# Two transformer blocks on one core: the 31-tap convolution as 64 four-tap matrices from memory, and the query block moved to the end of the input stage

## The chip, the cores and the metric

The kernel runs on one core of one Trainium2 chip. The metric is device time in microseconds (us) of one execution. The engines are named as in the profile: PE (TensorE), DVE (VectorE), ACT (ScalarE), POOL (GpSimd) and SP (SyncE, which here issues all DMAs). PEld is PE's weight load.

## The reference, cut to what matters

The kernel computes a first block of two layers and a second, different block of two layers, on 256 tokens of width 1024. The change is in the first block alone, between its input projection and its output projection:

```python
a = rmsnorm(h, norm_mix_pre[i])
u = einsum('bsd,de->bse', a, w_in[i])
q, k, v, qi, ki, wi, u_conv, u_pool = split(u)     # 512,128,128,1024,64,16,512,256
q, k, qi, ki = partial_rope(...)                   # first 16 of each 64 features
# index scores: relu(qi . ki) weighted by wi, summed over 16 heads; top 64 keys of each token
# attention of 8 heads over the selected keys
a_, g = split(u_conv)                              # 256 and 256
y = a_ * sigmoid(g)
y = depthwise causal convolution of y with 31 taps, 256 channels; + conv_b
y_conv = silu(layernorm(y)) @ conv_pw              # 256 x 256
# y_pool: window means over 2, 4, 8, 16 tokens less the input, then four 64 x 64 matrices
mix = concat([y_attn, y_conv, y_pool]) @ w_out
```

## The kernel before, in words

**Weights.** All weights stream through one queue of chunks of 128 x 2048 numbers, in the order in which they are used. SP loads each chunk in two halves of 512 KB into `raw` (two slots); ACT copies a half to `whi` in the reduced format fp32r (`prep`, line 490), DVE subtracts to get the rest `wlo` (`lo`, line 946); both have four slots. SP's load of chunk s waits for `lo` of chunk s-2, and `prep` of chunk s waits until PE is done with chunk s-4. A product of full precision is then three matmuls: high by high, high by low, low by high. `wide_block` does this with 512 columns of weights moving and 128 tokens as the stationary operand; `tile` does it with the weights stationary and 256 tokens moving. Products that don't involve streamed weights are plain fp32 matmuls, which the trace shows as two instructions each.

**Order.** Each engine has one program, written out by hand, and runs it in order; semaphores join them. Banks of PSUM (`acc` 0 to 3, `ub` 0 to 3) are handed on by `fill(bank, event)`: the next user of a bank waits for the event that the last use was given. In layer L of the first block the chunks are, counted from s0: 0 and 1 index key, key, value and the index weights; 2 to 5 the index queries; 6 and 7 the queries (`block_in(3, ...)`, by token halves into banks acc 2 and 3); 8 and 9 the convolution's input, 10 the pooling's (`pair_in`); then 11 to 14 the output projection ("out 0" to "out 3") and 15 on the feed-forward ("ffn 0" on).

**The stage of the change.** PE interleaves chunks 6 to 8 with the dots of the 16 index heads. ACT takes each head's relu, DVE adds it to the index sum (`index_sums`, line 1084). DVE rotates the queries (`rope(3)`, line 1073 on) in the middle of the index sums, and gates the convolution's input by ACT's sigmoid (`gated`) after the last index sum and in the search. The search for the 64 largest is eight rounds of MAX8 and MATCH_REPLACE8 (lines 1130, 1133). PE meanwhile runs chunk 9, turns the queries (`turn_in(3)`), runs chunk 10, the scores of heads 0 and 1, and 14 taps. Then comes a loop over eight heads: turn the probabilities (line 1891), scores of head hh+2 (lines 1818, 1819), values of head hh-1 (lines 1903 to 1907), and some taps. DVE masks the scores and takes the row maximum (lines 1152, 1156), ACT the exponent (line 637) and the copy of the turned probabilities (line 645).

**The convolution.** Channels lie on partitions, tokens along the row (`YC`, two units of 128 channels). A tap is a matmul of a diagonal 128 x 128 matrix with 256 shifted tokens (line 1929). POOL makes the diagonals, 46 a layer, in a ring of 16 (line 415), after the index dots, because they lie where the index queries lay; between the first 30 and the last 16 it does the pooling's window sums (lines 427 to 441). DVE does the other 16 taps itself (lines 1184, 1186), and a matmul by the identity adds them (line 1947). Mean, variance, spread of the reciprocal deviation and the pointwise convolution (lines 1953, 1968, 1977, 1987) follow on PE late in the loop and in the output projection.

## Time and profile before

| | |
|---|---|
| median of 3 runs | 2365.07 us (2364.63 to 2365.8) |
| the profiled execution: its time, its span | 2364.69 us, 2362.9 us |
| PE busy, PEld busy | 2336.6 us (99%), 1981.5 us (84%) |
| DVE, ACT, POOL busy | 1550.3 (66%), 1194.3 (51%), 118.8 (5%) us |
| granted TensorE clock | 9 (90% or more) in all 40 slices |
| HBM read | 424.05 MB, 180 GB/s over the span |
| chain that ended last | PE 88%, DVE 6%, POOL 2%, DMA 1%, ACT 1% |

The time of an execution is that of the whole program; the span runs from the first to the last instruction that the profile records. A matmul's record is longer than its slot, since matmuls are pipelined: what it costs in a row of them is the distance of the starts. A row with "x28" stands for 28 instructions in a row, its length reaches from the first's start to the last's modelled end. "[0.92 <-POOL ...]" is idle time before the row and what ended it.

### The profile page before, as it was taken

How to read it: one execution, taken by the hardware profiler on the slowest of the kernel's cores; microseconds unless marked ns; L12 is line 12 of the kernel's file. 1: busy time of each engine (PE TensorE's matmuls, PEld its weight loads, DVE VectorE, ACT ScalarE, POOL GpSimd, SP SyncE). 2: the span in 40 equal slices, each digit the busy share in tenths (PEclk: the TensorE clock that was granted, in tenths of full speed). 3: DMA queues.
4: the chain of work that ended last, by engine and by line, in shares of the span. 5: the costliest groups of instructions: out<-in, count | busy, mean ns of one | idle time of the engine just before them, and what ended most of it. 6: DMA issues, size and time to landing. Idle time of an engine off the chain costs nothing.

```text
span 2362.9 us, 30405 instructions
## 1 busy us (share of the span) xinstructions
PE 2336.6 (99%) x12096; PEld 1981.5 (84%) x12096; DVE 1550.3 (66%) x2041; ACT 1194.3 (51%) x1734; POOL 118.8 (5%) x223
## 2 busy tenths in 40 slices
PE   7999999999999999999999999999999999999998
PEld 6888888888888888988888888888889888888887
DVE  6866567866656656776485666665567765856664
ACT  6445446445445546545344455554565454444553
POOL 0500000500000000000000000000000000000000
PEclk9999999999999999999999999999999999999999
DMA  7236656236556665554656465565565445564563
GB/s 273 81 104 205 208 187 213 73 108 214 185 175 227 198 196 179 195 167 159 199 178 202 160 213 180 179 229 195 182 196 193 160 165 191 182 207 162 190 194 126
DMA packets 117501, 427.11 MB, mean 181 GB/s; under 512 B 13296, under 2 KB 13552, under 8 KB 117104
## 3 DMA queue, kind: packets, MB, share of 16 engines
q1 hardware_dynamic: 117360, 425.16, 54.7%
q8 instruction: 97, 1.59, 0.3%
q14 instruction: 44, 0.36, 0.0%
HBM read 424.05 MB, written 1.05 MB: 180 GB/s over the span
## 4 chain that ended last, share of the span: by engine, by line
PE 88%; DVE 6%; POOL 2%; DMA 1%; ACT 1%; issue 1%; SPq 0%; DVEq 0%; POOLq 0%; ACTq 0%
PE ub L1632 21%; PE ub L1636 11%; PE ub L1610 8%; PE ub L1612 8%; PE ub L1611 8%; PE acc L1610 8%; PE acc L1612 8%; PE acc L1611 8%; DVE wlo L946 2%; DMA raw<-in_w 1%; PE acc L1929 1%; POOL tapd L415 1%; DVE XN L987 1%; PE acc L2042 1%; ACT junk L512 1%
## 5 line engine op out<-in xcount | busy, mean ns | idle before, releaser
L946 DVE TENSOR_TENSOR wlo<-raw,whi 128x1024 fp32r<-128x1024 f32 x776 | 916.7, 1222 | 246.1 <-ACT whi L490 244.2
L490 ACT ACTIVATE whi<-raw 128x1024 fp32r<-128x1024 f32 x776 | 782.8, 1053 | 259.4 <-PE ub L1612 148.5
L1632 PE MATMUL ub<-xhl,whi 128*128 128x512 f32 x2176 | 595.2, 395 | 0.0
L1632 PEld LDWEIGHTS ub<-xhl,whi 128*128 128x128 f32 x2176 | 375.5, 189 | 53.5 <-issue 1.0
L1636 PEld LDWEIGHTS ub<-xhl,wlo 128*128 128x128 f32 x2176 | 333.5, 189 | 46.2
L1636 PE MATMUL ub<-xhl,wlo 128*128 128x256 f32 x2176 | 345.8, 281 | 0.0
L1610 PE MATMUL acc<-whi,bhl 128*128 128x512 f32 x736 | 288.6, 392 | 0.0
L1612 PE MATMUL acc<-whi,bhl 128*128 128x512 f32 x736 | 287.5, 391 | 0.0
L1611 PE MATMUL acc<-wlo,bhl 128*128 128x512 f32 x736 | 287.2, 390 | 0.0
L1610 PE MATMUL ub<-whi,xhl 128*128 128x512 f32 (+1 forms) x704 | 275.6, 391 | 7.8 <-DVE wlo L946 4.3
L1611 PE MATMUL ub<-wlo,xhl 128*128 128x512 f32 (+1 forms) x704 | 272.8, 387 | 0.0
L1612 PE MATMUL ub<-whi,xhl 128*128 128x512 f32 (+1 forms) x704 | 272.7, 387 | 0.0
L1610 PEld LDWEIGHTS ub<-whi,xhl 128*128 128x128 f32 x704 | 132.8, 189 | 36.5 <-DVE wlo L946 6.4
L1612 PEld LDWEIGHTS acc<-whi,bhl 128*128 128x128 f32 x736 | 138.1, 188 | 29.3
L1611 PEld LDWEIGHTS acc<-wlo,bhl 128*128 128x128 f32 x736 | 138.2, 188 | 27.4
L1610 PEld LDWEIGHTS acc<-whi,bhl 128*128 128x128 f32 x736 | 138.2, 188 | 27.1
L1612 PEld LDWEIGHTS ub<-whi,xhl 128*128 128x128 f32 x704 | 132.8, 189 | 26.6
L1611 PEld LDWEIGHTS ub<-wlo,xhl 128*128 128x128 f32 x704 | 132.9, 189 | 25.3
L1348 DVE TENSOR_TENSOR tX<-tS,ub 128x512 f32<-128x512 f32 x72 | 49.5, 688 | 137.3 <-ACT tS L773 136.8
L773 ACT ACTIVATE tS<-ub 128x512 f32<-128x512 f32 x72 | 42.9, 596 | 151.3 <-PE ub L1636 151.2
L1610 PE MATMUL ub<-whi,bhl 128*128 128x512 f32 x256 | 99.8, 390 | 0.0
L1612 PE MATMUL ub<-whi,bhl 128*128 128x512 f32 x256 | 99.6, 389 | 0.0
(311 smaller groups left out, 2578.5 us busy)
## 6 DMA issues: line engine op xcount, KB each, us to landing
raw<-in_w SPq DMA_DIRECT2D x776, 512.0 KB, 4.9
gain<-in_gains SPq DMA_DIRECT2D x20, 512.0 KB, 8.2
par<-in_par SPq DMA_DIRECT2D x2, 1068.0 KB, 9.4
DEC<-in_decay SPq DMA_DIRECT2D x2, 768.0 KB, 7.3
H<-in_x SPq DMA_DIRECT2D x2, 512.0 KB, 6.1
out_h<-H SPq DMA_DIRECT2D x4, 256.0 KB, 2.3
par<-in_par SPq DMA_DIRECT2D x2, 419.0 KB, 8.2
PT<-in_p SPq DMA_DIRECT2D x2, 256.0 KB, 8.4
```

The source lines that it names most:

```text
L415: do(pool.tensor_scalar(tapd[:, n % TAP_RING, :], ident, par1[:, P1["dw"] + n:P1["dw"] + n + 1], 1.0, ALU.mult, ALU.mult), taps)
L490: do(act.activation(whi[:, s % RING, c], raw[:, s % RAW, c], ACT.Copy), counts["w_hi"])
L512: do(act.activation(junk[:, :], H[:, t, fcol(fb)], ACT.Square, scale=1.0 / 32, accum_out=ssh[:, t, fb:fb + 1]), counts["ssh"])
L773: do(act.activation(units(tS[:, j % 2, :]), ub[:, 2 * (j % 2):2 * (j % 2) + 2, 0:S], ACT.Copy), counts["a_out"])
L946: do(dve.tensor_tensor(wlo[:, s % RING, c], raw[:, s % RAW, c], whi[:, s % RING, c].bitcast(f32), ALU.subtract), counts["w_lo"])
L987: do(dve.scalar_tensor_tensor(XN[:, fcol(fb)], H[:, t, fcol(fb)], rh[:, t:t + 1], gain[:, 1, fcol(fb)], ALU.mult, ALU.mult), counts["xn_re ...
L1348: do(dve.tensor_tensor(units(tX[:, j % 2, :]), units(tS[:, j % 2, :]), ub[:, 2 * (j % 2):2 * (j % 2) + 2, S:2 * S], ALU.add), counts["us"])
L1610: pe.matmul(o, x_h, w_h, start=first, stop=False, skip_group_check=True)
L1611: pe.matmul(o, x_h, w_l, start=False, stop=False, skip_group_check=True)
L1612: return pe.matmul(o, x_l, w_h, start=False, stop=last, skip_group_check=True)
L1632: pe.matmul(bank, whi[:, s % RING, n:n + P], xhl[:, kt, :, :].rearrange("p a n -> p (a n)"), start=kt == 0, stop=False, skip_group_check=True)
L1636: last = pe.matmul(bank[:, S:], wlo[:, s % RING, n:n + P], xhl[:, kt, 0, :], start=False, stop=kt == KT - 1, skip_group_check=True)
```

## The change

- The depthwise convolution is done for 64 channels at a time. Partitions 0 to 63 hold their even tokens, 64 to 127 their odd ones, each shifted by pairs: `YC` has four groups of 128 pairs. One 128 x 128 matrix, made on the host (`shifts`), holds up to four taps' entries: from even and odd input tokens to even and odd output tokens. Sixteen such matmuls of 128 columns make a group, 64 a layer. POOL's diagonals, DVE's own taps and the matmul that added them are gone.
- The matrices come from memory, in eight pieces of 512 KB a layer, through SP's queue and into a ring of four, two of which lie where the index queries and one where a projected block lay. SP waits, in its order, for those to be free and for earlier pieces to be used.
- The convolution's input is projected by token halves (`conv_in`, wide matmuls) from chunks 6 and 7, the pooling's from chunk 8, and the queries from chunks 9 and 10. The gated result is laid down by tokens (each 64 channels twice), turned by eight transposes (`turn_conv`), and ACT takes even tokens to the lower and odd tokens to the upper partitions (`even_and_odd`).
- DVE gates earlier, hands the pooling's input to POOL before the last three index sums, and rotates the queries after the search.
- PE's order after the dots: `turn_conv`, the query block, 14 taps, `turn_in(3)`, 10 taps, scores of heads 0 and 1, then the loop with 8 taps in each of the first five heads.
- Mean, variance, spread and pointwise convolution go by four groups of 128 columns. The variance comes out with tokens on partitions. The pointwise product uses 64 rows at a time, even tokens into bank ub 0 and odd into ub 1.

```diff
-TAP_RING = 16
+GROUPS = 4
+SHIFTS = 16
+PIECE = 8
+PIECES = GROUPS * SHIFTS // PIECE
+TAP_RING = 4
+PAIRS = S // 2
 RSPAN = 384
-TAPS_DVE = 16
-TAPS_BEFORE, TAPS_AFTER = 14, (7, 7, 6, 6, 6)
+TAPS_BEFORE, TAPS_AFTER = 24, (8, 8, 8, 8, 8)
...
-        tapd = sb("tapd", 0, at=unit(12), shape=[P, TAP_RING, P])
+        tapw = [sb(f"tapw{n}", 0, at=unit(u), shape=[P, PIECE, P]) for n, u in enumerate((32, 4, 12, 16))]
...
+        def load_taps(L, first, end):
+            for n in range(first, end):
+                k = PIECES * L + n
+                if n >= TAP_RING:
+                    sp.wait_ge(sem["tap_used"], k - TAP_RING + 1)
+                sp.dma_start(tapw[n % TAP_RING][:, :, :].rearrange("p a n -> p (a n)"),
+                             a["taps"][k * P:(k + 1) * P, :]).then_inc(sem[f"tap_in{n % TAP_RING}"], 16)
...
+                if s == s1(L, "inp", 10):
+                    if L:
+                        sp.wait_ge(sem["split_free"], s1(L - 1, "ple") + 1)
+                    load_taps(L, 0, 1)
+                if s == s1(L, "out", 2):
+                    sp.wait_ge(sem["ze"], 7 * L + 5)
+                    load_taps(L, 1, 2)
+                    sp.wait_ge(sem["dots_done"], IDX_HEADS * (L + 1))
+                    load_taps(L, 2, 5)
+                if s == s1(L, "out", 3):
+                    load_taps(L, 5, 6)
+                if s == s1(L, "ffn"):
+                    load_taps(L, 6, PIECES)
...
-            def tap_diagonals(start, end):
-                for n in range(start, end):
-                    if n >= TAP_RING:
-                        pool.wait_ge(sem["tap_used"], L * (2 * TAPS - TAPS_DVE) + n - TAP_RING + 1)
-                    do(pool.tensor_scalar(tapd[:, n % TAP_RING, :], ident,
-                                          par1[:, P1["dw"] + n:P1["dw"] + n + 1], 1.0, ALU.mult, ALU.mult), taps)
...
-            def sigmoid(f):
-                used(s0 + 8 + f)
-                do(act.activation(tS[:, f, 0:S], acc[:, f, S:2 * S], ACT.Sigmoid), counts["act_out"])
+            def sigmoid(t):
+                if t:
+                    used(s0 + 7)
+                else:
+                    nxt("cz")
+                do(act.activation(tS[:, t, 0:S], acc[:, 3 * t, S:2 * S], ACT.Sigmoid), counts["act_out"])
+            def even_and_odd(b):
+                nxt("yt_done")
+                for i in range(2):
+                    r = slice(64 * i, 64 * i + 64)
+                    src = acc[r, b, :].rearrange("p (g m i) -> p g m i", g=2, i=2)[:, :, :, i]
+                    do(act.activation(YC[r, 2 * b:2 * b + 2, SHIFTS - 1:], src, ACT.Copy),
+                       counts["yc_ready"] if i else None)
...
-            relus(4, 10)
+            relus(4, 7)
+            sigmoid(0)
+            relus(7, 10)
+            sigmoid(1)
             prep(s0 + 11)
+            relus(10, 16)
+            even_and_odd(0)
+            even_and_odd(1)
+            prep(s0 + 12)
             copy(3, 0)
+            prep(s0 + 13)
             copy(3, 1)
-            relus(10, 13)
-            sigmoid(0)
-            relus(13, 16)
-            prep(s0 + 12)
-            sigmoid(1)
-            prep(s0 + 13)
             turned_in(3)
...
-            def gated(f):
+            def gated(t):
                 nxt("act_out")
                 settle()
-                do(dve.tensor_tensor(YC[:, f, TAPS - 1:], acc[:, f, 0:S], tS[:, f, 0:S], ALU.mult),
-                   counts["in_free"])
+                x, y = (z.rearrange("p (g d) -> p g d", d=64).unsqueeze(2).broadcast_to([P, GROUPS, 2, 64])
+                        for z in (acc[:, 3 * t, 0:S], tS[:, t, 0:S]))
+                do(dve.tensor_tensor(YT[:, t, :, :, :], x, y, ALU.mult), counts["in_free"])
...
-            index_sums(4, 10)
+            index_sums(4, 7)
+            gated(0)
+            index_sums(7, 10)
+            gated(1)
             lo(s0 + 11)
-            rope(3)
-            index_sums(10, 16)
+            index_sums(10, 13)
             dve.wait_ge(sem["pads_ready"], L + 1)
-            gated(0)
+            used(s0 + 8)
+            do(dve.tensor_copy(UP[:, :, 16:], units(acc[:, 2, :])), counts["in_free"])
+            settle()
+            do(dve.memset(small[:, 0, 2:3], 0.0), counts["pool_in"])
+            index_sums(13, 16)
...
-                if r == 3:
-                    gated(1)
-            used(s0 + 10)
-            do(dve.tensor_copy(UP[:, :, 16:], units(acc[:, 2, :])), counts["in_free"])
-            settle()
-            do(dve.memset(small[:, 0, 2:3], 0.0), counts["pool_in"])
+            rope(3)
...
-            def own_taps(first, end):
-                for k in range(first, end):
-                    w = par1[:, P1["dw"] + TAPS + k:P1["dw"] + TAPS + k + 1]
-                    y = YC[:, 1, k:k + S]
-                    settle()
-                    if k == TAPS - TAPS_DVE:
-                        do(dve.tensor_scalar(CD[:, 0, :], y, w, None, ALU.mult))
-                    else:
-                        do(dve.scalar_tensor_tensor(CD[:, 0, :], y, w, CD[:, 0, :], ALU.mult, ALU.add),
-                           counts["cd_ready"] if k == TAPS - 1 else None)
...
+                    do(dve.tensor_scalar(cvar[:, :], acc[:, 3, 0:2], LN_EPS, None, ALU.add), counts["var_ready"])
...
+            do(dve.tensor_copy(spread[:, :, :], crs[:, :].unsqueeze(2).broadcast_to([P, 2, 64])),
+               counts["spread_ready"])
...
+            def conv_in(part, t):
+                s = s0 + 6 + part
+                if part == 0:
+                    fill(A_[3 * t], "in_free")
+                last = wide_block(s, 4 * part, t, acc[:, 3 * t, :], part == 0, part == 1, xhi, xlo)
+                if t:
+                    give(last)
+                elif part:
+                    give(last, "cz")
+            def pool_in(f):
+                arrive(s0 + 8, f)
                 if f == 0:
-                    fill(A_[n], "in_free")
+                    fill(A_[2], "in_free")
                 for kt in range(KT):
-                    last = tile(acc[:, n, f * S:(f + 1) * S], xhl[:, kt, :, :], s, f * KT + kt,
+                    last = tile(acc[:, 2, f * S:(f + 1) * S], xhl[:, kt, :, :], s0 + 8, f * KT + kt,
                                 kt == 0, kt == KT - 1)
                 if f:
                     give(last)
+            def turn_conv():
+                pe.wait_ge(sem["in_free"], 3 * L + 2)
+                for b in range(2):
+                    fill(A_[b], "yc_ready")
+                    for g in (2 * b, 2 * b + 1):
+                        for t in range(2):
+                            c = (g % 2) * S + t * P
+                            last = pe.transpose(acc[:, b, c:c + P],
+                                                YT[:, t, g, :, :].rearrange("p a d -> p (a d)"), ident)
+                    give(last, "yt_done")
...
-            block_in(3, 0, 0)
+            conv_in(0, 0)
             dots(0, 2)
-            give(block_in(3, 0, 1))
+            conv_in(0, 1)
             dots(2, 4)
             turn_in(2)
-            give(block_in(3, 1, 0), "xz")
+            conv_in(1, 0)
             dots(4, 7)
-            give(block_in(3, 1, 1))
+            conv_in(1, 1)
             dots(7, 10)
-            pair_in(s0 + 8, 0, 0)
+            pool_in(0)
             dots(10, 13)
-            pair_in(s0 + 8, 0, 1)
+            pool_in(1)
             dots(13, 16)
-            for f in range(2):
-                pair_in(s0 + 9, 1, f)
-            turn_in(3)
-            for f in range(2):
-                pair_in(s0 + 10, 2, f)
+            turn_conv()
+            both(3, 0)
+            both(3, 1)
...
             def taps(count):
                 for n in range(taken[0], taken[0] + count):
-                    f, k = divmod(n, TAPS)
+                    g, q = divmod(n, SHIFTS)
+                    piece, k = divmod(n, PIECE)
                     if n == 0:
                         fill(A_[3], "c_ready")
+                    if n % (2 * SHIFTS) == 0:
+                        pe.wait_ge(sem["yc_ready"], 2 * L + g // 2 + 1)
                     if k == 0:
-                        pe.wait_ge(sem["in_free"], 3 * L + 1 + f)
-                    pe.wait_ge(sem["tap_ready"], L * (2 * TAPS - TAPS_DVE) + n + 1)
-                    give(pe.matmul(acc[:, 3, f * S:(f + 1) * S], tapd[:, n % TAP_RING, :],
-                                   YC[:, f, k:k + S], start=k == 0, stop=f == 0 and k == TAPS - 1),
-                         "tap_used")
+                        pe.wait_ge(sem[f"tap_in{piece % TAP_RING}"], 16 * (2 * L + piece // TAP_RING + 1))
+                    last = pe.matmul(acc[:, 3, cols(g)], tapw[piece % TAP_RING][:, k, :], YC[:, g, q:q + PAIRS],
+                                     start=q == 0, stop=q == SHIFTS - 1)
+                    if k == PIECE - 1:
+                        give(last, "tap_used")
                 taken[0] += count
+            taps(TAPS_BEFORE - 10)
+            turn_in(3)
+            taps(10)
...
-                if hh == 4:
-                    nxt("cd_ready")
-                    give(pe.matmul(acc[:, 3, S:2 * S], ident, CD[:, 0, :], start=False, stop=True), "conv_done")
...
-                U_[1].take(pe, sem["prod_ready"], 4 * L + 4)
+                for place_ in U_[0:2]:
+                    place_.take(pe, sem["prod_ready"], 4 * L + 4)
                 for f in range(2):
-                    for k in range(2):
-                        c = P1["conv_pw"] + (k * 2 + f) * P
-                        last = pe.matmul(ub[:, 1, f * S:(f + 1) * S], par1[:, c:c + P], cact[:, k, :],
-                                         start=k == 0, stop=k == 1)
+                    for g in range(GROUPS):
+                        for j in range(2):
+                            r = slice(64 * j, 64 * j + 64)
+                            c = P1["conv_pw"] + (g * 2 + f) * P
+                            last = pe.matmul(ub[:, j, f * PAIRS:(f + 1) * PAIRS], par1[r, c:c + P],
+                                             cact[r, g, :], start=g == 0, stop=g == GROUPS - 1)
...
+def shifts(dw):
+    out = np.zeros((GROUPS, SHIFTS, 2, 64, 2, 64), np.float32)
+    c = np.arange(64)
+    for q in range(SHIFTS):
+        for i in range(2):
+            for j in range(2):
+                k = 2 * q + i - j
+                if 0 <= k < TAPS:
+                    out[:, q, i, c, j, c] = dw[k].reshape(GROUPS, 64)
+    out = out.reshape(PIECES, PIECE, P, P).transpose(0, 2, 1, 3)
+    return np.ascontiguousarray(out).reshape(PIECES * P, PIECE * P)
```

## Rows read from the trace of the kernel before

**Rows 1.** The page's busy time and share of the span by engine.
```profile
PE 2336.6 (99%) x12096; PEld 1981.5 (84%) x12096; DVE 1550.3 (66%) x2041; ACT 1194.3 (51%) x1734; POOL 118.8 (5%) x223
```

**Rows 2.** PE's waits, whole span: for whom; us in total, times, longest us.
```profile
PE acc L1929 <- POOL tapd L415: 1.8, 2, 0.9
```

**Rows 3.** PE's timeline, wide matmuls: start us, length us, engine, line, operation, count.
```profile
59.62 0.39 PE L1610 MATMUL acc<-whi,xhl 128*128 128x512 f32 x1
...
60.30 0.39 PE L1610 MATMUL acc<-whi,xhl 128*128 128x512 f32 x1
```

**Rows 4.** Timeline of PE from the index scores to head 5.
```profile
76.63 0.35 PE L1617 MATMUL acc<-xhl,whi 128*128 128x256 f32 x1 [0.40 <-ACT sm L590]
...
82.45 1.03 PE L1813 MATMUL ub<-cst,ZA 128*128 128x128 f32 x8
83.24 0.36 PE L1617 MATMUL acc<-xhl,whi 128*128 128x256 f32 x1
...
89.17 0.50 PE L1818 MATMUL ub<-KK,Q 64*128 64x128 f32 x4
...
90.03 6.31 PE L1929 MATMUL acc<-YC,tapd 128*128 128x256 f32 x28
96.19 0.49 PE L1891 MATMUL ub<-cst,sm 128*128 128x128 f32 x3
...
100.58 0.49 PE L1891 MATMUL ub<-cst,sm 128*128 128x128 f32 x3
...
102.57 3.24 PE L1929 MATMUL acc<-YC,tapd 128*128 128x256 f32 x14
...
121.35 0.49 PE L1891 MATMUL ub<-cst,sm 128*128 128x128 f32 x3
```

**Rows 5.** Timeline of PE in the second block: a head's scores and what follows.
```profile
1049.35 1.47 PE L2053 MATMUL acc<-q,k 128*128 128x256 f32 x8
1050.58 0.48 PE L1610 MATMUL ub<-whi,xhl 128*128 128x512 f32 x1
```

**Rows 6.** Timeline of VectorE: rotation, index sums, search, mask.
```profile
71.83 0.43 DVE L1073 TENSOR_TENSOR tX<-ZA,cc 128x256 f32<-128x256 f32 x1
...
73.22 2.45 DVE L1084 SCALAR_TENSOR_TENSOR iacc<-sm,wi,iacc 128x128 f32<-128x128 f32 x6
76.14 2.60 DVE L1084 SCALAR_TENSOR_TENSOR iacc<-sm,wi,iacc 128x128 f32<-128x128 f32 x6 [0.47 <-ACT sm L590]
...
79.33 0.62 DVE L1130 MAX8 best<-iacc 128x8 f32<-128x128 f32 x2
...
91.26 0.68 DVE L1138 COPY UP<-acc 128x512 f32<-128x512 f32 x1
...
93.15 0.56 DVE L1152 SCALAR_TENSOR_TENSOR sm<-ub,bias 128x384 f32<-128x384 f32 x1
```

**Rows 7.** POOL and VectorE together; third row: a line's ns min/median/max.
```profile
99.92 1.08 POOL L429 TENSOR_TENSOR W<-W 128x538 f32<-128x538 f32 x1
100.03 1.25 DVE L1186 SCALAR_TENSOR_TENSOR CD<-YC,par,CD 128x256 f32<-128x256 f32 x1
L1186 DVE SCALAR_TENSOR_TENSOR CD<-YC,par,CD x30: 483/485/1369, 100.0 to 466.7; 128x256 f32<-128x256 f32 x30
103.58 0.72 POOL L438 TENSOR_TENSOR PO<-W,cst 64x256 f32<-64x256 f32 x1
```

**Rows 8.** Timeline of ScalarE: two copies of a bank, end of head 0's exponent.
```profile
69.50 1.09 ACT L565 ACTIVATE ZA<-acc 128x512 f32<-128x512 f32 x2
...
95.19 0.18 ACT L637 ACTIVATION_READ_ACCUMULATOR sm<-sm,rmax 128x1 f32 x1
```

**Rows 9.** The page's DMA issues: count, KB each, median us to landing.
```profile
raw<-in_w SPq DMA_DIRECT2D x776, 512.0 KB, 4.9
```

**Rows 10.** Timeline of PE near the start: matmuls of 336 columns.
```profile
14.07 0.48 PE L1611 MATMUL ub<-wlo,xhl 128*128 128x336 f32 x1
14.35 0.48 PE L1612 MATMUL ub<-whi,xhl 128*128 128x336 f32 x1
```

More of the change, by code:

```diff
@@ L1951, in _ @@
                             fill(A_[3], "ha_ready")
-                            for k in range(2):
-                                last = pe.matmul(acc[:, 3, 0:S], means[:, :], cacc[:, k, :], start=k == 0, stop=k == 1)
+                            for g in range(GROUPS):
+                                last = pe.matmul(acc[:, 3, 0:PAIRS], means[:, :], cacc[:, g, :],
+                                                 start=g == 0, stop=g == GROUPS - 1)
                             give(last, "mean_done")
@@ L1966, in _ @@
                             fill(A_[3], "var_ready")
-                            for k in range(2):
-                                last = pe.matmul(acc[:, 3, 0:S], means[:, :], tS[:, 0, k * S:(k + 1) * S], start=k == 0, stop=k == 1)
+                            for g in range(GROUPS):
+                                last = pe.matmul(acc[:, 3, 0:2], tS[:, 0, cols(g)], means[:, 0:P:64],
+                                                 start=g == 0, stop=g == GROUPS - 1)
                             give(last, "stat_done")
@@ L1974, in last_values @@
                         turn_values(1)
-                        nxt("diag_ready")
+                        nxt("spread_ready")
                         fill(A_[3], "ha_ready")
-                        give(pe.matmul(rb, means[:, :], diag[:, :, :].rearrange("p a b -> p (a b)"), start=True, stop=True),
+                        give(pe.matmul(rb, spread[:, :, :].rearrange("p a b -> p (a b)"), ident, start=True, stop=True),
                              "rb_ready")
@@ L2250, in lay_out @@
         w_out = w_out.reshape(KT, P, D)[list(OUT_ORDER)].reshape(D, D)
-        w += [block_chunks(m) for m in (first, qi[:, 0:512], qi[:, 512:], q)]
-        w += [chunks(tiles(np.concatenate(last, axis=1))), column_chunks(w_out)]
+        w += [block_chunks(m) for m in (first, qi[:, 0:512], qi[:, 512:], conv)]
+        w += [chunks(tiles(pool)), block_chunks(q), column_chunks(w_out)]
         w += in_order({"first": block_chunks(v["w_up"][l][:, 0:1024]), "up": chunks(tiles(v["w_up"][l])),
@@ L2298, in lay_out @@
         "p": np.concatenate(ps, axis=0),
+        "taps": np.concatenate(taps, axis=0),
         "w": np.ascontiguousarray(np.concatenate(w, axis=0).reshape(-1, CHUNK)),
```

105 lines of the change are left out of this document (44 added, 61 removed).

## Prediction

> **What bounds the kernel now.** I read the page first: PE is busy for 99% of the span [rows 1]. A busy PE need not be a full one, so next came PE's waits. In the stretch that the change touches there are two a layer: 0.92 us for a diagonal that POOL makes [rows 2] and 0.40 us for an index relu [rows 4]. So PE's order of work is the clock of this kernel. A microsecond of PE work saved between the index scores and the out projection is a microsecond of the whole, as long as no other engine's result is late for PE. Last I read the timeline of each engine from 56 to 132 us, where the first layer does all this. The second layer repeats it with the same spacings (the wait on POOL has the same length in both [rows 2]), so I work out one layer and double it.
>
> **Prices.** A 512-column matmul of split numbers starts every 0.227 us (three in 0.68) [rows 3]; a 256-column one costs 0.123 (48 from 83.24 to 89.17, refill included) [rows 4]. A full-precision matmul is two instructions; with 256 columns each takes 0.22 (28 in 6.16 us) [rows 4]. With 128 columns: eight instructions of the second block's scores, four of 256 and four of 128 columns, take 1.23 us until the next matmul starts [rows 5]; less 4 x 0.22 that leaves 0.09 each. The weights must be loaded for each, and 0.12 is what a 256-column split matmul, as long in columns streamed, needs with its load. Ends 0.09 and 0.12; I take 0.108. A transpose costs 0.10 (eight in 0.79) [rows 4].
>
> **Up to the first softmax turn.** Before, PE is done with the index scores at 76.23 (76.63 less the wait) and begins turning head 0's probabilities at 96.19, a span of 19.96 us [rows 4]. What precedes 76.23 is the same work in other banks (four wide quarter blocks, one chunk of narrow tiles, 16 heads of dots), and I cost it at nothing. After it, one layer does this:
> - eight transposes of the gated convolution, 0.8, plus 0.1 for the switch: 77.15. The 0.40 us wait on the relu is covered by the first four.
> - 48 wide matmuls of the query block in place of two chunks of 48 narrow ones: 10.9 + 0.1, to 88.15 (the narrow ones took 11.9).
> - The taps write bank 3, which the second token half of the query block has just filled. They wait for ScalarE to copy it out: 0.28 until the last matmul lands beyond its slot, 0.55 for the copy (two in 1.09) [rows 8], and the semaphore. 0.9, a new wait: 89.05.
> - 14 taps, 28 x 0.108 = 3.0: 92.05.
> - Then the query block must be turned, and for that VectorE must have rotated it, which the change puts behind the top-64 search. This decides. Before, the index sums end at 78.74, the search runs from 79.33 to 91.26 with one gating of the convolution in it (0.5), so 11.45 bare; the rotation takes 1.39 (71.83 to 73.22) [rows 6]. The gatings and the copy of the pooling input leave this stretch and happen earlier, where VectorE has idle time. Without a delay: 78.75 + 11.45 + 1.4 = 91.6, in time for PE.
> - But the pooling input now reaches POOL at about 75.8 instead of 92, so that POOL's window sums, seven long tensor-tensor operations and more, run beside the last six index sums. The trace shows what that does: a VectorE operation with two SBUF inputs that began 0.11 us after a POOL sum of 1.08 took 1.25 us where the median of its 30 fellows is 0.485 [rows 7]: it ended 0.28 after the POOL operation it ran into. I take that for each. Walking the six index sums through a train of POOL's sums from 75.8 on (two of 1.08, then shorter ones, the sixth 0.72 [rows 7], those between taken as 0.75), they end at 81.6: 2.85 late. Search to 93.05, rotation to 94.45, PE resumes at 94.6, a wait of 2.5 us.
> - Turn the query block 0.8, ten taps 2.2, two heads' scores 0.9 (0.86 from 89.17 to 90.03): 98.5.
> - Nothing stands any more between the scores and the turn of head 0. Mask, row maximum and exponent take from 93.15 to 95.37 [rows 6, 8], with both semaphores 2.4: 100.9. Before, 14 taps hid this chain.
>
> So head 0 is turned 4.7 us later than before.
>
> The Trainium skill, in "SBUF — State Buffer", section "Who interferes with whom", says that a VectorE instruction with two SBUF inputs contends with a GpSimd instruction that reads SBUF, and that the second to start blocks until the first ends; with one SBUF input outside the two-port modes it doesn't. The pair of rows above agrees. The six index sums beside POOL's diagonals speak against it in size: 2.60 us instead of 2.45 [rows 6]. By the rule the sum stays at +4.7 us here, by that row it would be +2.2. By the same rule the search, which reads one SBUF input, isn't held up; no row here shows it beside POOL's long sums.
>
> **The loop over eight heads.** Before, 25.16 us from head 0's turn to head 5's [rows 4]. In it go 32 taps (64 x 0.22 = 14.1), the matmul that adds VectorE's taps (0.44) and the wait for the diagonals (0.92, with its refill 1.35) [rows 2]. In come 40 taps, 80 x 0.108 = 8.65. That is 7.2 us less. A head without taps costs 1.99 (100.58 to 102.57) [rows 4], with them 3.7. VectorE loses 16 taps of its own (0.485 us each in the median, up to 1.369) [rows 7], so mask, maximum and exponent of the next heads, at 1.25 + 1.0 us, keep ahead. POOL's 46 diagonals vanish from everybody's path. Four bias copies of 128 columns end 1.4 us after the last tap, the means come 2.4 after it: hidden.
>
> **The taps by DMA.** Eight pieces of 512 KB a layer come through SP's one queue, in order with the weights, ring of four. SP's waits for the index dots, for piece 0's use and so on stand ahead of the load of chunk out 3, which waits for VectorE's split of out 1 anyway, and that comes only after the second mask. So weights lose nothing. Pieces 0 to 4 land before use. Piece 5 is issued behind the two halves of out 3, some 4.9 us after the scores; such a load takes 4.9 us in the median from issue to landing [rows 9], it is wanted 11.2 us after the scores. Piece 6 is issued behind ffn 0 at 10.5 and wanted at 14.9: 4.4 us. With three transfers in flight I expect it 0.4 late; bounds 0 and 2.5. Piece 7 has 4 us more. The parameters grow by 228 KB, early, where PE waits for nothing that is behind them.
>
> **Layer norm and pointwise convolution.** Means: 8 instructions of 128 columns for 4 of 256, equal. Variance: 8 instructions with two columns, bound by their weight loads, equal. Spread: 0.2 shorter, but the wait behind it ends on ScalarE's silu, so nothing. Pointwise: 32 instructions of half the rows, in pairs on different row halves and banks, 16 slots x 0.108 = 1.73, for 8 of 0.22, 1.76. Do they not pair, 3.5. I take +0.2 with four silus for two. VectorE's own gain of 0.6 in the variance is hidden.
>
> **Sum.** A layer: +4.7 - 7.2 + 0.4 + 0.2 = -1.9 us; both: -3.8. The profiled execution took 2364.69 us, 1.8 around its span of 2362.9; it becomes 2360.9. It lay 0.4 under the median of the runs, so I predict 2361.3 us, 0.16% faster. A difference of 0.2%, 4.7 us, is about what can be told from none.
>
> **Rivals.**
> - *POOL holds nobody up.* For it: the six sums beside the diagonals. Against it: the rows of POOL's long sums. PE's wait of 2.5 us for the turn is gone: -4.4 a layer, 2356.2.
> - *Late pieces or an unpaired pointwise convolution.* Piece 6 and with it 7 late by 2.0 instead of 0.4, or 3.5 for 1.8: each +1.7 a layer, 2364.7. For the first: transfers queue in order and 2 MB are in flight. Against: the median of 4.9 us holds at the pace of the whole kernel, which keeps them busier than these 16 pieces do.
> - *The clock falls, slower than before.* The two waits of 2.5 and 2.4 us lie 3.9 us apart. Nothing like them follows the start in the trace of before. At the start matmuls of 336 columns come every 0.28 us, which is TensorE's lower level of 1.2 GHz; the later ones run at 2.4 [rows 3, 10]. If the first of the waits brings the level down, the 3.9 us of work between them double and the first head's 3.0 too: +6.9 a layer, 2375.1. With a fall after the second alone +3.0: 2367.3. It decides from the point where a wait is long enough for a fall, and nothing in this trace says where that is; the page's row of the clock is full throughout, and this counts a little against it.
>
> **Chances.** Forecast 0.44, no hold-up 0.22, late pieces or unpaired 0.16, clock 0.10, and 0.08 for a gain or loss of other size. The forecast's own spread is 2357.7 to 2364: the tap price between 0.09 and 0.12 alone gives -3.6 to +2.4 us over the 200 instructions that run after the search. Below 2360.3 lie 0.15 of the forecast, all of the second case and 0.03: faster 0.40. Above 2369.8 lies most of the clock case and a little else: slower 0.09. The rest, 0.51, is no difference. Range 2356 to 2367.
>
> **What would show it.** Right: tap instructions start every 0.11 us; PE waits of about 0.9, 2.5 and 2.4 us a layer ahead of the first tap, the turn of the query block and head 0's turn; six index sums that take over 5 us; no wait on POOL. Wrong: index sums of 2.5 us (second case), PE waiting for a tap piece over 1 us, or 512-column matmuls at 0.45 after the waits. If the search or masks run longer beside POOL, the first wait grows with it.

## The result: slower by 0.56%, and the profile after

The changed kernel takes 2378.01 us in the median of four runs (2374.87 to 2381.53), the one before 2364.86 (2364.63 to 2365.80) beside it: a ratio of 1.0056, 95% interval [1.0044, 1.0068]. The forecast was 2361.3 us, with a range up to 2367.0. Not only the median is off. The runs of before lie within 1.2 us, those of the changed kernel within 6.7, and that spread is a finding by itself. Two executions lie far outside all others, one of the kernel before at 2898.38 us and one of the kernel with filled waits below at 6054.48; they are left out of the ratios and move no median by more than 0.1 us.

The page of the changed kernel: busy time of the engines, and two DMA groups (count, KB each, median us from issue to landing). They answer to [rows 1] and [rows 9].

```profile
PE 2330.5 (98%) x12148; PEld 1977.6 (83%) x12148; DVE 1532.4 (65%) x2005; ACT 1199.5 (51%) x1750; POOL 70.2 (3%) x133
...
raw<-in_w SPq DMA_DIRECT2D x776, 512.0 KB, 4.9
tapw<-in_taps SPq DMA_DIRECT2D x16, 512.0 KB, 6.5
```

PE is busy 6.1 us less, while the span grew by 12.1 us, from 2362.9 to 2375.0. So PE waits 18.2 us more. PE's waits after 40 us (for whom; us in total, times, longest):

```profile
PE acc L1964 <- DMA tapw<-in_taps: 6.1, 4, 3.1
PE ub L1824 <- DVE ZA L1104: 4.9, 2, 2.5
PE ub L1923 <- ACT sm L664: 4.6, 2, 2.3
...
PE acc L1621 <- ACT ZB L578: 2.7, 1, 2.7
PE ub L2027 <- issue: 2.0, 2, 1.0
PE acc L1964 <- ACT ZA L578: 1.4, 2, 0.7
```

Lines two, three and six are the waits that the prediction worked out (2.5, 2.4 and 0.9 a layer, found 2.46, 2.30 and 0.69). Lines one and four are not in it at those sizes. The wait on the diagonals [rows 2] is gone. In the kernel before, the same view has no wait above 0.9 us after 40 us.

PE's timeline of the first layer (start us, length us, what; in brackets the idle time before it), which answers to [rows 4]:

```profile
52.41 0.50 PE L1621 MATMUL acc<-whi,xhl 128*128 128x512 f32 x1 [2.66 <-ACT ZB L578]
...
54.48 0.63 PE L1622 MATMUL acc<-wlo,xhl 128*128 128x512 f32 x1
54.91 0.63 PE L1623 MATMUL acc<-whi,xhl 128*128 128x512 f32 x1
...
80.44 1.09 PE L1869 MATMUL acc<-cst,YT 128*128 128x128 f32 x8
93.12 3.39 PE L1964 MATMUL acc<-YC,tapw 128*128 128x128 f32 x28 [0.69 <-ACT ZA L578]
98.97 1.09 PE L1824 MATMUL ub<-cst,ZA 128*128 128x128 f32 x8 [2.46 <-DVE ZA L1104]
...
105.46 0.55 PE L1923 MATMUL ub<-cst,sm 128*128 128x128 f32 x3 [2.30 <-ACT sm L664]
...
114.83 2.05 PE L1964 MATMUL acc<-YC,tapw 128*128 128x128 f32 x16 [0.17 <-DMA tapw<-in_taps]
...
121.97 3.67 PE L1964 MATMUL acc<-YC,tapw 128*128 128x128 f32 x16 [3.10 <-DMA tapw<-in_taps]
...
129.30 0.49 PE L1923 MATMUL ub<-cst,sm 128*128 128x128 f32 x3
...
136.97 0.48 PE L1621 MATMUL acc<-whi,bhl 128*128 128x512 f32 x1
...
144.36 2.06 PE L2027 MATMUL ub<-cact,par 64*128 64x128 f32 x32 [0.98 <-issue]
```

Read it from the bottom up. The out projection starts at 136.97 where it started at 128.97 before, 8.0 us late. Two things happen that nobody ordered: the convolution's first matmul waits 2.66 us, and the 16 tap instructions at 121.97 last 3.67 us where the 16 at 114.83 last 2.05. The 512-column matmuls from 54.06 on stand 0.43 us apart, where they stood 0.227 apart [rows 3]. 512 columns in 0.43 us are 1.2 GHz, the lower level of TensorE's clock. The windows of the same trace say it outright (stretch, length; busy us of PE, PEld, DVE, ACT, POOL; granted clock; DMA share; GB/s):

```profile
52.00:54.00 2.00, 1.59 (x6) 1.34 (x7) 1.90 (x4) 2.00 (x5) 0.00 (x0) 0.93 0.94 363
54.00:56.00 2.00, 2.00 (x6) 1.55 (x5) 1.70 (x4) 1.71 (x2) 0.00 (x0) 0.50 0.88 315
56.00:58.00 2.00, 2.00 (x11) 1.02 (x11) 1.16 (x2) 0.13 (x1) 0.00 (x0) 0.72 1.00 385
...
122.00:124.00 2.00, 2.00 (x9) 2.00 (x10) 0.00 (x0) 0.00 (x0) 0.00 (x0) 0.50 0.94 315
124.00:126.00 2.00, 2.00 (x13) 1.83 (x11) 0.00 (x0) 0.00 (x0) 0.00 (x0) 0.65 0.55 199
```

The seventh number is the granted clock as a share of full speed. It falls to 0.50 behind the wait of 2.66 us, behind the one of 3.10, and in layer 1 behind that of 2.49 us for the same tap piece (472 to 478 us). What a fall costs can be estimated as the missing share of the clock times PE's busy time in each window: 0.11 + 1.0 + 0.56 = 1.7 us for the first, 1.0 + 0.7 = 1.7 for the second, 1.5 for the third, 4.9 us in all. The 16 tap instructions above agree: 3.67 us for 2.05 is 1.6 more. In the kernel before, no window of 2 us shows less than 1.00 before PE's last instruction. The page's row of the clock rounds these falls away: it is full in both kernels, since a slice is 59 us long.

### The profile page after: what moved, and what is told of

It is laid out like the page before. It is cut to its first block, busy times and chain, and to the rows that moved or that the text cites. A ratio compares the mean times of both kernels' runs of the same rounds, so it can differ in the third digit from the quotient of the medians.

```text
span 2375.0 us, 30415 instructions
## 1 busy us (share of the span) xinstructions
PE 2330.5 (98%) x12148; PEld 1977.6 (83%) x12148; DVE 1532.4 (65%) x2005; ACT 1199.5 (51%) x1750; POOL 70.2 (3%) x133
## 3 DMA queue, kind: packets, MB, share of 16 engines
HBM read 432.91 MB, written 1.05 MB: 183 GB/s over the span
## 4 chain that ended last, share of the span: by engine, by line
PE 87%; DVE 7%; DMA 2%; ACT 1%; POOL 1%; issue 1%; SPq 0%; DVEq 0%; POOLq 0%; ACTq 0%
PE ub L1643 21%; PE ub L1647 11%; PE ub L1621 8%; PE ub L1622 8%; PE ub L1623 8%; PE acc L1621 7%; PE acc L1623 7%; PE acc L1622 7%; DVE wlo L973 2%; DMA raw<-in_w 2%; PE acc L1964 1%; DVE XN L1014 1%; DMA tapw<-in_taps 1%; PE acc L2082 1%; ACT junk L525 1%
```

## The experiments

The kernel before was run beside each of them: medians of 2364.7 to 2364.8 us. The first four undo or mend one thing each of the changed kernel, and differences are against its 2378.0.

**The tap pieces earlier.**

```diff
                             sp.wait_ge(sem["dots_done"], IDX_HEADS * (L + 1))
-                            load_taps(L, 2, 5)
+                            load_taps(L, 2, 7)
                         if s == s1(L, "out", 3):
-                            load_taps(L, 5, 6)
-                        if s == s1(L, "ffn"):
-                            load_taps(L, 6, PIECES)
+                            load_taps(L, 7, PIECES)
```

> Only the order of the tap loads changes: pieces 5 and 6 are issued ahead of the chunk out 3 and piece 7 ahead of ffn 0, where the changed kernel issues each one chunk later. My theory: piece 6 was late because 1.5 MB stood in the queue with it and ahead of it, and the wait (3.10 us in layer 0, 2.49 in layer 1) brought the clock down for the 16 tap matmuls behind it (3.67 us for 1.84). Then both go: 3.1 + 2.5 + 2 x 1.8 and the two small waits for piece 5 (0.17, 0.29) = 9.7 us less than the changed kernel, 2368 us against its 2378, and the out projection of layer 0 starts 5 us earlier. Rival: the queue has no room, so the weights of out 3 and ffn 0 come late instead and the wait turns into one for the low halves of the weights: 3 us less or nothing, 2375 to 2378.

Measured: 2370.61 us (2365.53 to 2375.61, ten runs), ratio 1.0024 [1.0015, 1.0034], 7.4 less. PE waits for no piece any more in the trace, and no new wait on weights came; the rival is out. The median landing of a piece fell from 6.5 us to 4.4. That the gain isn't the expected 9.7, and that ten runs spread over 10 us, goes with the clock. In the profiled execution (2371.63 us) it fell in other places: in layer 0 behind the 2.30 us wait for the exponent, which had left it alone in the changed kernel's profile, and for longer (windows below); in layer 1 behind waits of 2.47 and 2.31 us. By the sum used above these three falls cost 8.2 us. The times of the ten runs follow their mean granted clock: 0.999 in those of 2365.5 and 2366.2 us, 0.995 in the three of 2372.6 to 2375.6.

```profile
102.00:104.00 2.00, 1.61 (x6) 1.28 (x7) 1.97 (x4) 1.30 (x7) 0.00 (x0) 0.54 0.13 49
104.00:106.00 2.00, 2.00 (x8) 1.35 (x7) 1.83 (x4) 0.39 (x2) 0.00 (x0) 0.50 0.34 98
106.00:108.00 2.00, 2.00 (x12) 2.00 (x11) 0.60 (x2) 0.98 (x4) 0.00 (x0) 0.50 0.90 299
108.00:110.00 2.00, 2.00 (x11) 1.38 (x10) 0.00 (x0) 0.49 (x1) 0.00 (x0) 0.75 0.50 186
```

**Another bank for the convolution's first half.**

```diff
-                            fill(A_[3 * t], "in_free")
-                        last = wide_block(s, 4 * part, t, acc[:, 3 * t, :], part == 0, part == 1, xhi, xlo)
+                            fill(A_[2 + t], "in_free")
+                        last = wide_block(s, 4 * part, t, acc[:, 2 + t, :], part == 0, part == 1, xhi, xlo)
...
-                            fill(A_[2], "in_free")
+                            fill(A_[0], "in_free")
...
-                            last = tile(acc[:, 2, f * S:(f + 1) * S], xhl[:, kt, :, :], s0 + 8, f * KT + kt,
+                            last = tile(acc[:, 0, f * S:(f + 1) * S], xhl[:, kt, :, :], s0 + 8, f * KT + kt,
```

The sigmoid, the gating and the copy of the pooling input read the new banks.

> Only banks are exchanged: the first token half of the convolution's block goes to accumulator bank 2 (and the second stays in bank 3), the pooling's to bank 0, so that the first wide matmuls of the convolution needn't wait for ScalarE to copy the third block out of bank 0. My theory: this wait (2.66 us, layer 0 only) and the low clock behind it (512-column matmuls at 0.43 us) are all of the 4.2 us by which the index scores of layer 0 end late: 80.4 becomes 76.3, the total 2378 becomes 2374. Rival: the larger parameters (647 KB a load for 419) and the first piece make the weights late here; then the wait moves to the weights of the convolution's block and at most 1 us is gained.

Measured: 2374.28 us (2370.68 to 2380.49, six runs), ratio 1.0041 [1.0028, 1.0054], 3.7 less. PE's timeline of this kernel: the convolution starts at once, and the transposes behind the index scores come at 76.37, where they came at 80.44 in the changed kernel and the scores ended at 76.23 before.

```profile
49.67 0.48 PE L1621 MATMUL acc<-whi,xhl 128*128 128x512 f32 x1
...
76.37 1.09 PE L1869 MATMUL acc<-cst,YT 128*128 128x128 f32 x8
```

So the larger parameters and the first piece cost nothing here, and the bank, with the fall behind it, was all of the 4.2 us. The execution as a whole took 2378.04 us all the same: the clock fell five times in it, behind waits of 2.13 to 2.83 us, for 10.3 us by the same sum.

**GpSimd's signal behind the last index sums.**

```diff
                     do(dve.tensor_copy(UP[:, :, 16:], units(acc[:, 2, :])), counts["in_free"])
+                    index_sums(13, 16)
                     settle()
                     do(dve.memset(small[:, 0, 2:3], 0.0), counts["pool_in"])
-                    index_sums(13, 16)
```

> Only the signal that lets GpSimd begin its window sums moves, from ahead of VectorE's last six index sums to behind them. My theory: those six take 2.5 us in place of 5.62 and the top-64 search, which reads one SBUF input, takes 11.4 beside GpSimd's sums as before; the rotation ends some 2.9 us earlier and PE's wait for it (2.46 us in each layer) is gone: 2 x 2.46 = 4.9 less, 2378 becomes 2373. Rival: GpSimd disturbs the search as well; each of its two-input sums of 1.08 us holds an instruction of the search, the search takes 13 to 14 us and PE's wait stays at 2 us or more: under 1 us of gain.

Measured: 2371.59 us (2369.28 to 2376.02, six runs), ratio 1.0032 [1.0020, 1.0044], 6.4 less. First VectorE and GpSimd in the changed kernel, then in this one; they answer to [rows 6] and [rows 7]:

```profile
80.22 1.09 POOL L441 TENSOR_TENSOR W<-UP 128x542 f32<-128x542 f32 x1 [63.42 <-DVE small L1156]
...
80.41 5.62 DVE L1111 SCALAR_TENSOR_TENSOR iacc<-sm,wi,iacc 128x128 f32<-128x128 f32 x6 [0.34 <-ACT sm L603]
86.06 0.62 DVE L1165 MAX8 best<-iacc 128x8 f32<-128x128 f32 x2
```

```profile
78.51 2.45 DVE L1111 SCALAR_TENSOR_TENSOR iacc<-sm,wi,iacc 128x128 f32<-128x128 f32 x6 [0.47 <-ACT sm L603]
...
81.12 0.62 DVE L1165 MAX8 best<-iacc 128x8 f32<-128x128 f32 x2
...
81.23 1.09 POOL L441 TENSOR_TENSOR W<-UP 128x542 f32<-128x542 f32 x1 [64.04 <-DVE small L1157]
...
92.69 0.42 DVE L1100 TENSOR_TENSOR tX<-ZA,cc 128x256 f32<-128x256 f32 x1
```

The six sums take 5.62 us beside GpSimd's and 2.45 without it. The search behind them runs from 81.12 to 92.6 with GpSimd beside it for 8.4 us and is no longer than it was bare, 11.5. PE's wait of 2.46 us is gone in both layers. The gain is larger than the 4.9 us of wait that went; the rest lies within the spread that the clock makes. The Trainium skill, "SBUF — State Buffer", section "Who interferes with whom", tells the two kinds of VectorE instruction apart in just this way, and the trace now agrees with both halves of it.

**Taps behind the first scores.**

```diff
-                    taps(10)
+                    taps(4)
                     scores(0)
                     scores(1)
+                    taps(6)
```

> Only six of the ten taps that stand ahead of the scores of heads 0 and 1 are moved behind them. My theory: PE's wait for the mask, maximum and exponent of head 0 (2.30 us in each layer) is a chain that begins with the scores, which now come 1.4 us earlier; 0.9 of the wait is left: 2 x 1.3 = 2.6 us less, 2378 becomes 2375. Rival: the scores then wait for ScalarE's two copies of the turned queries, which six of the ten taps had hidden; then PE waits 0.5 us more there and the gain is 1.6; if the chain isn't bound by the scores but by VectorE's masks behind the rotation, it is 0.

Measured: 2372.17 us (2369.30 to 2375.91, five runs), ratio 1.0033 [1.0020, 1.0046], 5.8 less. The wait is 0.50 in layer 0 (with low clock up to 101 us, which stretches PE's work ahead of it) and 0.8 in layer 1, 1.3 in all for 4.6. No wait for the queries' copies appeared. The gain is larger than the 3.3 us of wait that went; the rest lies within the spread that the clock makes.

**Waits filled with work that nobody needs.** This separates the clock from the waits.

```diff
+                        if hh == 0:
+                            pe.wait_ge(*U_[2].free)
+                            for _ in range(18):
+                                pe.transpose(ub[:, 2, 0:P], ident, ident)
                         nxt("exp_ready")
```

That is the place ahead of head 0's turn; the three others are alike.

> The changed kernel with all its waits, but PE fills the four kinds of long wait with transposes of a constant into a bank that nobody reads: 20 (2.0 us) ahead of the convolution's first matmuls in layer 0, and in each layer 20 ahead of the turn of the query block, 18 ahead of head 0's turn, 22 and 18 ahead of tap piece 6. Nothing becomes available earlier. My theory: idle PE is what brings the clock down; with it busy the clock stays full, the waits end when they did, and the half-speed stretches are gone: 5 us less in the median (2373) and a spread under 2 us instead of 6.7. Rival: the clock falls for another reason, or hardly costs anything: time as the changed kernel, 2378, and the same spread; or the transposes last longer than the waits and it is slower still.

Measured: 2371.28 us, ratio 1.0027 [1.0016, 1.0038], 6.7 less, and the eight runs compared lie within 3.1 us; granted clock 0.999 to 1.000 in each, where the changed kernel had 0.993 to 0.998. The expectation of 2373 was 1.7 too high; its 5 us of low clock came from the profiled execution, which was itself 1.2 us faster than the median.

> The kernel whose long waits are filled with transposes once more, for its trace: where the changed kernel's trace shows a clock of 0.50 behind a wait of 2.5 to 3.1 us, this one shows 1.00 throughout, and the operations that ended those waits (the copy of the third block, the rotation, the exponent, tap piece 6) end when they did. If the clock falls for another reason, windows of 0.50 remain.

Its trace (2370.42 us): PE's timeline around the wait for the rotation, and two windows in which the changed kernel showed 0.50.

```profile
94.02 2.35 PE L1815 MATMUL ub<-cst 128*128 128x128 f32 x20
96.65 1.09 PE L1828 MATMUL ub<-cst,ZA 128*128 128x128 f32 x8 [0.28 <-DVE ZA L1104]
```

```profile
54.00:56.00 2.00, 2.00 (x14) 1.21 (x13) 1.67 (x2) 0.82 (x3) 0.00 (x0) 1.00 0.89 299
...
122.00:124.00 2.00, 2.00 (x17) 1.77 (x16) 1.52 (x5) 0.42 (x3) 0.00 (x0) 1.00 0.59 197
```

The turn still comes 5.86 us behind the first tap (96.65 and, not shown, 90.79), as in the changed kernel (98.97 - 93.12 = 5.85), but PE is idle for 0.28 us of it in place of 2.46. No window shows less than 1.00 between 40 us and PE's last instructions. So idle PE is what brings the clock down here.

The 6.7 us are not all the clock's, though, since two things came earlier in this execution (rows not shown). ScalarE's copy of the third block began at 50.28 us in place of 51.77, so that the stretch ahead of the convolution took 2.10 us for 2.66; and tap piece 6 held PE up 0.8 us less in layer 0 and 0.3 less in layer 1. With 0.2 more for piece 5 that makes 1.4 of the 6.4 us by which this span (2368.6) is shorter than the changed kernel's. The 5.0 that are left match the 4.9 which the windows of the changed kernel add up to.

**The four mends together.**

> The four earlier edits together: tap pieces issued earlier, the convolution's first half in bank 2 and the pooling in bank 0, GpSimd's signal behind the last index sums, six taps behind the first scores. My theory: four waits of 2.3 to 3.1 us, each of which may bring the clock down for 3.4 or 6.9 us, are what makes the changed kernel slow; here they go or shrink below 1 us, so the granted clock is full through both layers, and against the profile of the changed kernel (2376.8) it saves 2.5 for the bank, 6.1 for the pieces, 4.9 and 2.7 for the two chains and 5.0 of low clock: 2355.6 us, 0.4% faster than before, with runs that lie within 1.5 us of each other. Rival: the falls have little to do with these waits or another wait takes their place (VectorE's masks, the weights): 2362 or more.

Measured: 2355.05 us (2354.44 to 2355.59, five runs), ratio 0.9958 [0.9946, 0.9971]: 23.0 less than the changed kernel and 9.7 less than before, with the spread of before. Of its waits the longest after 40 us are 1.0 and 0.8 us, and no window between 40 us and PE's last instructions shows less than full clock. Its timeline, head 0's turn, 16 taps, head 5's turn:

```profile
97.18 0.55 PE L1921 MATMUL ub<-cst,sm 128*128 128x128 f32 x3 [0.76 <-ACT sm L662]
...
110.04 2.00 PE L1962 MATMUL acc<-YC,tapw 128*128 128x128 f32 x16
111.88 0.49 PE L1921 MATMUL ub<-cst,sm 128*128 128x128 f32 x3
...
115.71 0.49 PE L1921 MATMUL ub<-cst,sm 128*128 128x128 f32 x3
```

**One long wait put back at a time.** The next two kernels are this one with one mend undone: first GpSimd's signal, then the order of the ten taps.

> The kernel with all four edits, less one: GpSimd's signal stands ahead of the last six index sums again, so that PE has one long wait a layer (about 2.5 us for the rotated queries) and no other above 1 us. My theory: a single such wait is enough to bring the clock down in a part of the executions: 4.9 us for the waits themselves, and 0 to 3.4 us for one or two falls of 1.7 us each; 2360 to 2363, runs spread over more than 2 us, granted clock 0.997 to 0.999. Rival: the falls need two waits close behind each other; then the time is 2355.05 + 4.9 = 2360.0 with a spread of 1 us and a full clock.

Measured: 2360.80 us (2359.84 to 2363.18, eleven runs), ratio 0.9986 [0.9977, 0.9995]; 5.75 more than all four for 4.9 us of waits. The three runs with a mean granted clock of 1.000 took 2359.84 to 2360.80 us, the three with 0.998 took 2362.76 to 2363.18.

> The kernel with all four edits, less another: all ten taps stand ahead of the first scores again, so that PE waits some 2.3 us a layer for head 0's mask, maximum and exponent and nowhere else above 1 us. My theory: 2 x 1.5 for the wait, which was 0.8 a layer in the kernel with all four, less 0.2 for the queries' copy, is 2.7 us, and the clock falls behind this wait in a part of the executions for up to 1.7 us each, or 3.4 where it stays low twice as long: 2358 to 2362, spread over 2 us. Rival: 2.3 us are too short for a fall by themselves: 2357.8, spread of 1 us.

Measured: 2360.68 us (2359.83 to 2363.29, eleven runs), ratio 0.9984 [0.9975, 0.9993]; 5.6 more for 3.1 us of waits (4.6 for 1.5). Granted clock 0.998 in each of its eleven runs. Windows of the first, behind its wait in layer 0, and of the second, in layer 1, with the line of its timeline that ends the wait:

```profile
94.00:96.00 2.00, 0.83 (x4) 0.83 (x5) 1.90 (x7) 0.00 (x0) 0.00 (x0) 0.75 0.04 16
96.00:98.00 2.00, 2.00 (x11) 2.00 (x10) 0.04 (x1) 1.40 (x3) 0.00 (x0) 0.50 0.00 0
98.00:100.00 2.00, 2.00 (x16) 1.55 (x16) 0.41 (x1) 1.07 (x1) 0.00 (x0) 0.89 0.47 150
```

```profile
443.05 0.90 PE L1921 MATMUL ub<-cst,sm 128*128 128x128 f32 x3 [2.30 <-ACT sm L662]
```

```profile
444.00:446.00 2.00, 2.00 (x6) 1.35 (x7) 1.87 (x3) 0.69 (x3) 0.00 (x0) 0.50 0.15 51
446.00:448.00 2.00, 2.00 (x12) 2.00 (x11) 0.86 (x3) 0.99 (x4) 0.00 (x0) 0.50 0.86 270
448.00:450.00 2.00, 2.00 (x11) 1.70 (x11) 0.00 (x0) 0.11 (x1) 0.00 (x0) 0.58 0.58 213
```

A single wait of 2.3 to 2.5 us can be enough; both rivals, that it takes two or that 2.3 is too short, are out. From the turn of head 0 to that of head 1 the second kernel needs 449.03 - 443.05 = 5.98 us in layer 1, where the clock fell, and 102.25 - 99.03 = 3.22 in layer 0, where it didn't behind the same wait of 2.30 us: that fall costs 2.8.

**The best version.** The four mends, one more tap behind the scores, and the pointwise convolution one unit later:

```diff
-                        if i == 4:
+                        if i == 5:
                             conv_out()
```

> The kernel with all four edits and two more: seven taps in place of six behind the first scores, and the pointwise convolution one unit of the out projection later (ahead of the sixth in place of the fifth). My theory: the 0.97 us that PE waits in each layer for the four silus is covered by the 1.4 us of that unit, less 0.2 that the split of its result then comes late, and 0.2 of the 0.8 us in front of head 0's turn goes: 2355.05 - 2 x 1.0 = 2353.0 us. Rival: the split of the pointwise convolution's result (1.4 us on VectorE) is what the out projection then waits for, as long as before: 2355, no change.

Measured: 2353.03 us (2352.67 to 2354.51, five runs), ratio 0.9952 [0.9938, 0.9965]. It is 2.0 us below the version with four mends, as expected; the wait of 0.97 us a layer is gone, and the one for the exponent is 0.5. It beats both kernels: 0.5% below the one before, 1.05% below the changed one.

## Why the prediction was wrong

Between the forecast of -3.8 us and the +12.1 of the profiled execution lie 15.9. By the steps of the prediction:

- **"What precedes 76.23 ... I cost it at nothing"** failed, for 4.2 us. The convolution's first half goes into bank 0, which the third block's first half has just filled, and ScalarE copies that out behind a weight chunk that arrives late. The timeline of ScalarE, first before, then in the changed kernel:

```profile
50.43 1.07 ACT L565 ACTIVATE ZB<-acc 128x512 f32<-128x512 f32 x2
```

```profile
50.81 1.06 ACT L503 ACTIVATE whi<-raw 128x1024 fp32r<-128x1024 f32 x1 [1.23 <-DMA raw<-in_w]
51.77 1.07 ACT L578 ACTIVATE ZB<-acc 128x512 f32<-128x512 f32 x2
```

  PE wants the bank at 49.75. With the first of the two copies done at 51.0 that is a wait of over a microsecond even by the old times; the chunk came later still and made it 2.66. Before, the next block went into a bank that had been free for long. "The same work in other banks" isn't free until each new bank's last reader is looked up. The fall of the clock behind it (1.7 us) is inside the 4.2. This execution was a bad one: with the same banks the traces of the earlier pieces, of GpSimd's signal and of the taps behind the first scores have waits of 1.60, 1.93 and 1.68 us here, and no fall behind them.
- **"Piece 6 ... I expect it 0.4 late; bounds 0 and 2.5"** was a term mis-sized. Pieces 5 to 7 were late by 6.05 us in all for 0.8 forecast. SP's queue of the changed kernel shows why (start us, length us, issues):

```profile
112.42 1.46 SPq L307 DMA_DIRECT2D raw<-in_w  x2
113.92 0.91 SPq L319 DMA_DIRECT2D tapw<-in_taps  x2
```

  Piece 6 is issued 1.5 us behind the two halves of a chunk and lands around 121.9, 8 us later. The median of 4.9 us [rows 9] is that of the steady pace, two halves at a time; behind 1 MB that was issued just before, with half a megabyte of its own, it doesn't hold. With the pieces issued earlier and nothing else changed their median is 4.4; in the other kernels with that order it is 4.5 to 5.8, in those with the old order 6.3 to 6.8.
- **"The clock falls, slower than before"** was the rival with 0.10, and it happened, though not where it was placed: in the profiled execution behind the waits that I hadn't forecast (4.9 us with the one counted above, 3.2 without it), in others behind those that I had. Filling the waits gave back 6.7 us in the median, and of the 6.4 between the two traces 5.0 are the clock's. The reason against it was that nothing in the trace of before said where the point is and that its row of the clock was full. The first was no reason for a small chance: that trace has no wait above 0.9 us after the first 40 us, so it couldn't show a fall at any length. The Trainium skill, "TensorE: Matmul & The Clock Gate", section "HAM oscillation — how this bites in real kernels", warns that waits between bursts of matmuls can bring the clock down each time anew; the traces here agree, with a fall behind 20 of the 28 waits of 2.1 to 3.1 us in the seven of them that have any after 40 us. The forecast, which had two such waits a layer on its own account, should have given this rival the largest weight after itself.
- **Up to head 0's turn, +4.7 a layer**, was right: 80.44 to 105.46 is 25.02 us in place of 19.96, +5.06. The delay of the six index sums (2.85 forecast, 5.62 - 2.45 = 3.17 found), the wait of 2.46 for the rotation, the exponent's 2.30 and the bank's 0.69 are all there. "POOL holds nobody up" is out. Over both layers this adds 0.7.
- **The loop, -7.2 a layer**, was right in kind. Without falls and late pieces it takes 115.71 - 97.18 = 18.53 us, -6.6. A tap instruction starts every 0.115 us (16 in 1.84) and not every 0.108. +1.1 for both layers.
- **Pointwise convolution, +0.2** became +0.9 a layer. It pairs (32 instructions in 1.99 us up to the next matmul, 1.62 for the eight before), so that rival of mine is out; but the four silus take 1.65 us for 1.09, and PE waits 0.98 for them in place of 0.21. I had put the two silus more under the same 0.2, without a time for them from any row. +1.5 for both.

4.2 + 5.2 + 3.2 + 0.7 + 1.1 + 1.5 = 15.9, the missing 15.9. That it closes to the tenth is luck, because two things that are in no item cancel. The loop's 1.1 is read from the kernel with four mends; in the changed kernel the loop takes 23.84 and 23.36 us (105.46 to 129.30, and in layer 1 457.42 to 480.78), which is 0.9 more for both layers than 18.53 each with the waits for pieces and the falls added. And behind the second layer's pointwise convolution the changed kernel is 12.9 us late (497.82 for 484.92), at its end 12.1; what makes up these 0.8 us was not looked into.

The order of cause: late pieces and a bank brought waits of over 2 us; they and the two that were forecast let the clock fall; that turned a gain of fixed size into a loss that varies from run to run. What the change was to bring is there once the waits are shortened: -9.7 us, and -11.7 in the best version.

What stays open is what decides whether a given wait brings a fall and how long it lasts: behind the same wait of 2.30 us the clock stayed full in one layer and was low for 6 us in the other. No run was made for that.

## What to carry to other kernels

A wait of over 2 us on a TensorE that is otherwise always busy costs its length and, behind 20 of 28 such waits here, an estimated 1.4 to 3.4 us more for work at the lower clock; so when a reordering leaves such a wait, put work of its own into it (six taps moved behind the scores took 2.30 us down to 0.5 to 0.8), and judge the change by several runs, since its spread is the sign. When a block moves to another accumulator bank, look up who reads that bank last and what stands ahead of that reader on its engine. And a load's median landing time holds for the place in the queue at which it was measured: issue an added load as soon as its buffer is free, ahead of the next large one and not behind it.

## What the runs showed of the hardware

- TensorE's granted clock falls from 1.00 to 0.50 behind a single wait, but not behind each of the same length. In the seven traces with waits of 2.13 to 3.10 us after 40 us it fell behind 20 of 28; both outcomes are there for 2.30 and for 2.46 us. Of four waits of 1.48 to 1.93 us one brought a fall, that of 1.48 (for tap piece 6 in layer 1, with the taps behind the first scores). How long it stays low differs: back to full between 124 and 126 us after a fall at 122 in the changed kernel, not before 108 after one at 102 with the earlier pieces. Waits of 1.05 us and less, with PE busy around them, brought none in any of the traces.
- Transposes of a constant in the wait keep it up as well as useful matmuls do: 0.999 to 1.000 in all timed runs.
- At the start the windows of every trace show 1.00 while the 336-column matmuls stand 0.28 us apart [rows 10], 1.2 GHz. There the spacing tells the level and the clock's column doesn't.
